# Routing stage of a two-block network on one core: choosing among 112 sums, dealing one-hot tiles singly, and moving three expert tiles and two weight loads

## The reference, cut to what matters

```python
def peer(h, wq, subkeys, u_tab, v_tab):          # 512 tokens, in blocks of 128
    q = (hb @ wq).reshape(128, 8, 2, 128)        # 8 heads, two halves
    s = einsum('thsd,snd->thsn', q, subkeys)     # 128 scores for each half
    s1, i1 = top_k(s[:, :, 0], 16)
    s2, i2 = top_k(s[:, :, 1], 16)
    cand = (s1[..., :, None] + s2[..., None, :]).reshape(..., 256)
    sc, ci = top_k(cand, 16)                     # 16 of 256 sums, for each head
    e1 = take_along_axis(i1, ci // 16); e2 = take_along_axis(i2, ci % 16)
    idx, gate = e1 * 128 + e2, softmax(sc)
    act = gelu(hb @ u_tab[idx].T) * gate
    return act @ v_tab[idx]
```

## Time and profile before

| | us |
|---|---|
| three runs | 4666.91, 4678.98, 4681.0 |
| median | 4678.98 |
| profiled execution: its own time | 4670.62 |
| its span | 4668.7 |
| first choice, VectorE, from 1096.1 | 39.8 |
| spreading, units 0 to 127 | 1137.9 to 1411.4: 273.5 |
| from there to the first `down` matmul | to 1445.9: 34.5 |

### The profile page before, as it was taken

The page is one execution under the profiler, slowest core; times in us unless marked ns, Lnnn a source line. Parts: engine busy times, 40 slices in busy tenths (PEclk is TensorE's granted clock), DMA queues, the critical chain, the costliest instruction groups (busy, mean ns, idle before and its releaser), DMA issues.

```text
span 4668.7 us, 51767 instructions
## 1 busy us (share of the span) xinstructions
PE 4338.2 (93%) x20942; PEld 3394.4 (73%) x20942; DVE 2612.5 (56%) x4338; ACT 1508.5 (32%) x2520; POOL 1928.1 (41%) x1031
## 2 busy tenths in 40 slices
PE   7878999998778999999999989988999989988999
PEld 3667755467666888888888877677888867756886
DVE  4675755458775888878645442653533450364334
ACT  3211311024773322222222232653222231353222
POOL 2244423134884555555555443104322236334443
PEclk9998999998889999999999999999999999999999
DMA  6200310332235454554554420001212212102321
GB/s 217 81 32 1 117 34 28 113 128 70 106 145 203 162 171 167 167 167 162 172 170 162 142 84 19 24 1 55 68 59 64 68 37 66 39 1 74 99 91 54
DMA packets 171050, 445.52 MB, mean 95 GB/s; under 512 B 12251, under 2 KB 79003, under 8 KB 167612
## 3 DMA queue, kind: packets, MB, share of 16 engines
q1 hardware_dynamic: 168060, 422.61, 27.1%
q0 software_dynamic: 2752, 19.60, 1.1%
HBM read 404.41 MB, written 37.75 MB: 95 GB/s over the span
## 4 chain that ended last, share of the span: by engine, by line
PE 71%; DVE 5%; ACT 4%; POOL 2%; issue 2%; DMA 0%; SPq 0%; POOLq 0%; ACTq 0%; DVEq 0%
PE psum L254 20%; PE psum L255 20%; PE psum L256 19%; PE psum L260 11%; PE psum L355 1%; POOL Pe L2579 1%; POOL Pd L2581 1%; DVE o L1591 1%; ACT o L1656 0%; ACT o L1659 0%; ACT stage L1665 0%; POOL pair L244 0%; DMA raw_ring<-peerv 0%; DVE oh L1560 0%; DVE ci L1542 0%
## 5 line engine op out<-in xcount | busy, mean ns | idle before, releaser
L244 POOL TENSOR_TENSOR pair<-raw_ring,pair 128x1024 fp32r<-128x1024 f32 x502 | 1304.5, 2607 | 1947.0 <-ACT pair L236 1894.4
L236 ACT CAST pair<-raw_ring 128x1024 fp32r<-128x1024 f32 x502 | 517.2, 1048 | 742.8 <-PE psum L256 687.6
L254 PE MATMUL psum<-pfh,pair 128*128 128x512 f32 x1152 | 459.8, 399 | 4.9 <-DVE pfl L1501 3.4
L255 PE MATMUL psum<-pfl,pair 128*128 128x512 f32 x1152 | 457.6, 397 | 0.0
L256 PE MATMUL psum<-pfh,pair 128*128 128x512 f32 x1152 | 452.6, 393 | 0.0
L1775 DVE SCALAR_TENSOR_TENSOR hlate<-psum,mods,hlate 128x512 f32<-128x512 f32 x512 | 367.1, 747 | 131.6 <-PE psum L256 129.7
L254 PE MATMUL psum<-Ah,pair 128*128 128x512 f32 x1024 | 402.3, 393 | 16.0 <-DVE Al L1769 16.0
L255 PE MATMUL psum<-Al,pair 128*128 128x512 f32 x1024 | 404.2, 395 | 0.0
L256 PE MATMUL psum<-Ah,pair 128*128 128x512 f32 x1024 | 398.0, 389 | 0.0
L254 PE MATMUL psum<-ffh,pair 128*128 128x512 f32 (+1 forms) x1056 | 377.6, 358 | 18.4 <-DVE ffl L1941 15.7
L255 PE MATMUL psum<-ffl,pair 128*128 128x512 f32 (+1 forms) x1056 | 377.0, 357 | 0.0
(11 more groups left out here) (616 smaller groups left out, 8848.6 us busy)
## 6 DMA issues: line engine op xcount, KB each, us to landing
raw_ring<-wmod SPq DMA_DIRECT2D x144, 512.0 KB, 5.4
raw_ring<-peeru SPq DMA_DIRECT2D x128, 512.0 KB, 3.5
raw_ring<-peerv SPq DMA_DIRECT2D x128, 512.0 KB, 3.8
gates<-stage SPq DMA_DIRECT2D x16, 2048.0 KB, 6.3
Gb<-gates SPq DMA_DIRECT2D x32, 1024.0 KB, 9.6
raw_ring<-win SPq DMA_DIRECT2D x48, 512.0 KB, 4.4
raw_ring<-wgate SPq DMA_DIRECT2D x44, 512.0 KB, 3.5
raw_ring<-wup SPq DMA_DIRECT2D x44, 512.0 KB, 3.5
```

The costliest lines, as they stand in the source:

```text
L236: ac.e.copy(self.pair(t)[0], k.R.of(t)).then_inc(*k.A.up("hi", t))
L244: po.e.tensor_tensor(lo, k.R.of(t), hi.bitcast(F), ALU.subtract).then_inc(*k.G.up("lo", t))
L254: e.matmul(out, w[0], x[0], start=first, stop=False, skip_group_check=True)
L255: e.matmul(out, w[0], x[1], start=False, stop=False, skip_group_check=True)
```

## The change

Four things change.

1. The choice looks at 112 sums of a head instead of 256: all 16 columns for the first four rows, and four columns for rows 4 to 15. They are made in sixteen smaller additions instead of eight. Since the place no longer is row times 16 plus column, nine small VectorE instructions work out row and column where four did; they are a piece of their own.
2. The owner of an `o1` tile is dealt for each token, not for each unit. `deal()` keeps a running load for each engine, adds to it the engine's other work of the unit, and gives each tile to the engine with the least.
3. Three U tiles (U8, U9, U10 behind units 2, 34 and 66) stay beside the spreading. U11 to U16 come after it.
4. SyncE loads V0 and V1 after the tenth store of gates, and V2 and V3 after the last store and ahead of loading the gates back.

```diff
-BESIDE = {2 + 16 * (n - FIRST): n for n in range(FIRST, EARLY)}
+BESIDE = {2: 8, 34: 9, 66: 10}
+CHOICE = 1.62
...
-            pe.wait_ge({"fused": G, "vector": V, "scalar": A}[own_o1(u)].at("o1", u, i2))
+            pe.wait_ge({"pool": G, "vector": V, "scalar": A}[OWN[4 * u + i2]].at("o1", u, i2))
...
-def own_o1(u):
-    if u >= 96:
-        return ("fused", "vector", "vector", "scalar", "fused", "vector", "vector")[u % 7]
-    i = u % 32 - u % 32 // 16
-    return "vector" if u % 16 == 15 else "scalar" if 13 * i % 30 < 13 else "fused"
+def deal():
+    cost, load, out = {"pool": 0.84, "scalar": 0.87, "vector": 0.29}, {"pool": 0.0, "scalar": 0.0, "vector": 0.0}, []
+    for u in range(128):
+        load["vector"] += CHOICE if u < 96 else 0.68
+        load["scalar"] += 0.58
+        if u in BESIDE:
+            load["scalar"] += 1.65
+            load["pool"] += 2.35
+        for i in range(4):
+            n = min(cost, key=lambda n: load[n] + cost[n])
+            load[n] += cost[n]
+            out.append(n)
+        if u == 95:
+            load = dict.fromkeys(load, 0.0)
+    return out
+OWN = deal()
...
-        for hd in range(8):
-            c = k.cand[:, 256 * hd:256 * hd + 256]
-            e.tensor_tensor(v3(c, 16), ... ALU.add)      # 16 x 16
-            if hd % 2:
-                yield
+        for lo, hi, w, at in ((0, 4, 16, 0), (4, 16, 4, 64)):
+            for hd in range(8):
+                o = c3[:, hd, at:at + w * (hi - lo)].rearrange("p (i j) -> p i j", j=w)
+                e.tensor_tensor(o, ... ALU.add)          # 4 x 16, then 12 x 4
+                if hd % 4 == 3:
+                    yield
...
-            if s == 0:
-                e.tensor_scalar(k.hiU, k.ci, 4, None, ALU.logical_shift_right)
-            else:
-                e.tensor_scalar(k.hiU, k.ci, 15, None, ALU.bitwise_and)
-            e.tensor_copy(k.hiF, k.hiU)
+        e.tensor_scalar(k.hiU, k.ci, 4, None, ALU.logical_shift_right)
+        e.tensor_copy(place, k.ci)
+        e.tensor_copy(row, k.hiU)
+        e.tensor_scalar(k.hiU, k.ci, 2, None, ALU.logical_shift_right)
+        e.tensor_copy(tmp, k.hiU)
+        e.scalar_tensor_tensor(out=row, in0=tmp, scalar=-12.0, in1=row, op0=ALU.add, op1=ALU.max)
+        e.tensor_scalar(tmp, row, 4.0, 48.0, ALU.mult, ALU.add)
+        e.scalar_tensor_tensor(out=tmp, in0=row, scalar=16.0, in1=tmp, op0=ALU.mult, op1=ALU.min)
+        e.tensor_tensor(place, place, tmp, ALU.subtract)
+        yield
...
-    for n in range(EARLY, AHEAD):                        # PE, ACT and POOL, behind the spreading
+    for n in range(FIRST + len(BESIDE), AHEAD):
...
         if ch == 0:
             R.load(sp, ("U", AHEAD - 1))
+        if ch == 9:
+            R.load(sp, ("V", 1))
+    R.load(sp, ("V", 3))
     sp.wait_ge(k.stl[0].at(8), k.stl[1].at(8))
```

More of the change, by code:

```diff
@@ L1517, in choose @@
         f4 = k.fidx[:, tt, :].rearrange("p (h s k) -> p h s k", h=8, s=2)
-        for hd in range(8):
-            c = k.cand[:, 256 * hd:256 * hd + 256]
-            e.tensor_tensor(v3(c, 16), bc(v4_[:, hd, 0, :], 2, [128, 16, 16]), bc(v4_[:, hd, 1, :], 1, [128, 16, 16]), ALU.add).then_inc(*V.up())
-            if hd % 2:
-                yield
-        groups = [tuple(x[:, w * hd:w * hd + w] for x, w in ((k.cand, 256), (k.best, 16), (k.ci, 16), (k.oh, 256))) for hd in range(8)]
+        c3 = v3(k.cand[:, 0:896], 112)
+        for lo, hi, w, at in ((0, 4, 16, 0), (4, 16, 4, 64)):
+            for hd in range(8):
+                o = c3[:, hd, at:at + w * (hi - lo)].rearrange("p (i j) -> p i j", j=w)
+                shape = [128, hi - lo, w]
+                e.tensor_tensor(o, bc(v4_[:, hd, 0, lo:hi], 2, shape), bc(v4_[:, hd, 1, 0:w], 1, shape), ALU.add).then_inc(*V.up())
+                if hd % 4 == 3:
+                    yield
+        groups = [tuple(x[:, w * hd:w * hd + w] for x, w in ((k.cand, 112), (k.best, 16), (k.ci, 16), (k.oh, 112))) for hd in range(8)]
         for half in (groups[0:4], groups[4:8]):
@@ L1547, in choose @@
         o4 = v4(k.oh, 16, 16)
-        for s in range(2):
-            if s == 0:
-                e.tensor_scalar(k.hiU, k.ci, 4, None, ALU.logical_shift_right).then_inc(*V.up())
-            else:
-                e.tensor_scalar(k.hiU, k.ci, 15, None, ALU.bitwise_and).then_inc(*V.up())
+        place, row, tmp = k.cand[:, 0:128], k.cand[:, 128:256], k.cand[:, 256:384]
+        e.tensor_scalar(k.hiU, k.ci, 4, None, ALU.logical_shift_right).then_inc(*V.up())
+        e.tensor_copy(place, k.ci).then_inc(*V.up())
+        dv.wait_ge(V.now())
+        e.tensor_copy(row, k.hiU).then_inc(*V.up())
+        dv.wait_ge(V.now())
+        e.tensor_scalar(k.hiU, k.ci, 2, None, ALU.logical_shift_right).then_inc(*V.up())
+        dv.wait_ge(V.now())
+        e.tensor_copy(tmp, k.hiU).then_inc(*V.up())
+        dv.wait_ge(V.now())
+        e.scalar_tensor_tensor(out=row, in0=tmp, scalar=-12.0, in1=row, op0=ALU.add, op1=ALU.max).then_inc(*V.up())
+        dv.wait_ge(V.now())
+        e.tensor_scalar(tmp, row, 4.0, 48.0, ALU.mult, ALU.add).then_inc(*V.up())
+        dv.wait_ge(V.now())
+        e.scalar_tensor_tensor(out=tmp, in0=row, scalar=16.0, in1=tmp, op0=ALU.mult, op1=ALU.min).then_inc(*V.up())
+        dv.wait_ge(V.now())
+        e.tensor_tensor(place, place, tmp, ALU.subtract).then_inc(*V.up())
+        yield
+        for s, which in ((0, row), (1, place)):
             dv.wait_ge(V.now())
-            e.tensor_copy(k.hiF, k.hiU).then_inc(*V.up())
-            dv.wait_ge(V.now())
-            e.tensor_tensor(o4, bc(v3(k.hiF, 16), 3, [128, 8, 16, 16]),
+            e.tensor_tensor(o4, bc(v3(which, 16), 3, [128, 8, 16, 16]),
                             k.row["i16"].unsqueeze(1).unsqueeze(1).to_broadcast([128, 8, 16, 16]), ALU.is_equal).then_inc(*V.up())
@@ L1591, in vector_route @@
         e.tensor_tensor(v3(k.o2[n], 128), *marks(k, u), ALU.is_equal).then_inc(*V.up("o2", u))
-        if own_o1(u) == "vector":
-            for i in range(4):
-                q = 4 * u + i
+        for i in range(4):
+            q = 4 * u + i
+            if OWN[q] == "vector":
                 e.tensor_scalar(k.o1[n][:, 128 * i:128 * i + 128], S["iota"], k.EG[0][:, q:q + 1], k.EG[2][:, q:q + 1], ALU.is_equal,
@@ L1652, in gates @@
         q = 4 * u
-        if own_o1(u) == "scalar":
+        mine = [i for i in range(4) if OWN[q + i] == "scalar"]
+        if mine:
             ac.wait_ge(V.at("EG", u // 32), P.at("sp", u - NO) if u >= NO else None)
-            for i in range(4):
+            for i in mine:
                 e.activation(o[i], k.sq["iota"], AF.Abs, scale=-1.0, bias=k.EG[0][:, q + i:q + i + 1]).then_inc(*A.up())
             ac.wait_ge(A.now())
-            for i in range(4):
+            for i in mine:
                 e.activation(o[i], o[i], AF.Relu, scale=k.EG[3][:, q + i:q + i + 1], bias=k.EG[2][:, q + i:q + i + 1]).then_inc(*A.up("o1", u, i))
@@ L1702, in pool_route @@
             W.lo(po, ("U", BESIDE[u]))
[L1703 to L1706, removed]
+        for i in range(4):
+            q = 4 * u + i
+            if OWN[q] == "pool":
+                po.wait_ge(V.at("EG", u // 32), P.at("sp", u - NO) if u >= NO else None)
                 e.tensor_scalar(k.o1[n][:, 128 * i:128 * i + 128], S["iota"], k.EG[0][:, q:q + 1], k.EG[2][:, q:q + 1], ALU.is_equal,
@@ L1827, in rounded @@
         e.copy(k.Ah[n % 4], k.pr[n % 3]).then_inc(*A.up("Ah", n))
-    for n in range(EARLY, AHEAD):
+    for n in range(FIRST + len(BESIDE), AHEAD):
         up(n)
```

## The result

The changed kernel takes 4624.65 us (median of four runs, 4621.01 to 4632.57), where the kernel before takes 4677.32 in the same runs: ratio 0.9882, 95% interval 0.9847 to 0.9917. I had said 4650 with a range of 4628 to 4668. The profiled execution took 4624.38 us, its span 4622.6, 46.1 less than before, twice the 21.8 that my terms add up to. (The medians differ by 52.7.)

What follows compares the result with a forecast made beforehand. TensorE was taken to bound the kernel (71% of the span), gains coming only where the chain leaves it. Terms -3.5 - 22 - 0.7 + 4.4 = -21.8 on 4670.6 gave 4648.8, stated as 4650, range 4628 to 4668.

Steps and rivals of the forecast that it cites:

- First choice, -3.5: First choice, ahead of the spreading: gate ready at 1132.3 instead of 1135.9, ScalarE's exponential ending last; -3.5 us, bounds -3 and -3.6.
- Blocks 0 to 2, -22: First three spreading blocks: 70.5 us each, -8 each and -6 for block 0; -22 us together, bounds -40 and -5.
- Only four units of buffers lie between engines: Blocks 0 to 2: reason for reckoning each block in three phases, 24.5, 24.0 and 17.5 us, sum 66.0.
- Taking away the second one: Blocks 0 to 2: removing a block's second U tile, in the slow phase, frees 0 to 2 us.
- Of which dealing gives little back: Blocks 0 to 2: first U tile costs 8.3 less 3.6 us, 4.7, and dealing recovers little of that.
- Block 3, -0.7: Last spreading block: VectorE drops to 59 tiles, GpSimd rises to 46, 38.9 us; -0.7 us, bounds -3 and +3.
- Handover, +4.4: Last spreading matmul (E) to first `down`: E+39.0 instead of E+34.5, six U tiles following; +4.4 us, bounds +2 and +9.
- Ports: Spreading: VectorE and GpSimd share ports; added cost to GpSimd at most some 4 us a block; wrong if its tile exceeds 1 us.
- Nothing left of it: Rival 1, blocks 0 to 2: queues stay out of step, blocks at 76, total 4670; chance 0.13.
- slower: Rival 2, blocks' first phase: VectorE's piece and other engines' tiles add, 24 us a block; 4685 at half; chance 0.06.
- half clock: Rival 4, blocks: TensorE's clock stays at 1.2 GHz, 3 us a block, 4659; chance 0.08.
- Even dealing works fully: Rival 3, spreading: `deal()` loads of 57.6 a block and 38.9 for the last hold, 4610; chance of below 4632: 0.13.

## Why the prediction was wrong, step by step

**First choice, -3.5: right**, -3.4, and for the reason given: the exponential behind the GELU of U7 ended last.

**Blocks 0 to 2, -22: this is the step that failed**, -46.9. I added up three phases, each at the pace of its slowest engine. In block 1 that gave 70.7 us, taken as 70.5, where 62.2 were measured; 7.1 of the difference lie in the third phase, 17.5 for 10.4. Three statements behind it went wrong.
- "Only four units of buffers lie between engines, so that a slow phase can't be averaged with a fast one." They can in part. GpSimd needs neither VectorE's `o2` nor its piece; in the slow phase it started 20 tiles where those 8 units hold 17. Three buffers instead of four cost 2.4 to 3.3 us a block, which shows that the lead counts.
- "Taking away the second one ... frees little (0 to 2)." Alone it freed 6.4 us in block 1, 6.1 of them in the third phase. With the tile there, GpSimd made a remainder in the slow phase (2.36 us) and stood still for TensorE as the third began (4.33). My check of the reckoning on the kernel before hid this: its third phase of 19.0 us looked like 11 units at 1.75 and was a stalled one.
- "Of which dealing gives little back." Undoing it costs 6.5 us a block on average, doing it alone gives 7.5. I had priced it at the 3.6 us of unit 34 and at nothing for the other turns. My block 1 went from 78.4 to 70.7 us by 3.4 for the shorter choice, 0.7 for the second U tile and these 3.6; alone the three measured 6.6, 6.6 and 7.5 a block.

What held: the middle phase (24.1 against 24.0), the first phase with its U tile (27.7 against 29.2), VectorE's shorter pieces, and GpSimd's load as the limit. For that limit I had taken 65 us a block as the far bound, though the text gave 63.5 for GpSimd's own work; it was 61.6. Three blocks at 65 are 38 us less than before, at 63.5 they are 43 less; measured were 46.9. So the bound -40 was too near.

**Block 3, -0.7: within its bounds**, +1.5. GpSimd is the bound there (40.90 of 41.70 busy), as the term had it, at 826 ns a tile. But 50 of its tiles start in this stretch, not 46: it had four of block 2 left when VectorE began block 3. A block bounded by VectorE's starts doesn't hold just its own tiles of GpSimd.

**Handover, +4.4: right in size** (+5.2; to `down` 39.8 us behind E where I had 39.0), with both gaps where they were put. The gap at U13 was 1.57 instead of 1. The `Gb` load was covered, by 10 us instead of 7: the gates came back 25.8 us behind E, not 28.

**Ports.** GpSimd's tile grew neither beyond 1 us nor at all in the changed kernel, 924 ns; so the shared ports of the Trainium skill's "SBUF — State Buffer", section "SBUF: two separate sides", show no added cost in the mean. Inside a block the cost is seen: in block 1 GpSimd's tiles take 0.81 us on average in the first phase, 1.19 beside VectorE's long passes and 0.80 in the third.

**Rivals.** "Nothing left of it", "slower" and "half clock" did not come; the granted clock rose in each of the blocks 0 to 2, from 0.75, 0.83 and 0.83 to 0.79, 0.89 and 0.87. "Even dealing works fully" (4610) was the nearest: the blocks came to 62 where `deal()` says 57.6. GpSimd's true cost of a tile, 0.92 with the long passes against the 0.84 that `deal()` uses, makes 5 us of difference for 66 tiles.

**What stays open.** How much of the 16 us a block belongs to which part has no single answer, since they overlap: alone 6.6, 7.5 and 6.6 us a block (choice, dealing, U tiles), undone 4.6, 6.5 and 5.8. What the early loads are worth with three U tiles behind the spreading was not isolated. Why the last store of gates landed later in some traces, and why block 2 varies by 2 us, was not tried.

## What to carry to other kernels

Before giving a phase its slowest engine's time, ask which other engines may run on in it: the sum over a block is bounded by the greatest total load of one engine, and that bound must be inside the range whenever an edit evens out the work. A part that only makes work fit together (dealing by tile instead of by unit) has no cost in any row; its price can be as much as the idle time of the bound engine, here 11.5 us a block, of which the dealing alone gave 7.5. And parts that remove the same idle time need not add: 56.6 us alone, 43.6 together in these traces.

## What the runs showed of the hardware

A copy of 128 columns on VectorE took ten times its usual time when GpSimd's subtraction of a weight tile (SBUF to SBUF) was running. VectorE, then GpSimd, in order of time in the first choice of the kernel after:

```profile
1108.16 0.23 DVE L1572 CAST cand<-hiU 128x128 f32<-128x128 uint32 x1
...
1108.68 2.32 DVE L1576 CAST cand<-hiU 128x128 f32<-128x128 uint32 x1
```

```profile
1108.45 2.46 POOL L244 TENSOR_TENSOR pair<-raw_ring,pair 128x1024 fp32r<-128x1024 f32 x1 [3.08 <-ACT pair L236]
```

The same copy two instructions earlier takes 0.23. The Trainium skill, "SBUF — State Buffer", section "SBUF: two separate sides", has the shared ports as an exclusive lock: whichever of the two engines starts first keeps them for its whole instruction. The trace agrees, since the copy ends 0.1 us behind the subtraction; that the copy ran in a mode that takes these ports is not shown. VectorE's one-hot tiles meet the same at units 2, 34 and 66, beside GpSimd's remainder: 2.38, 2.02 and 2.41 us for one tile, where the median is 0.34. An `o2`, which reads one of its inputs from PSUM, was not held up: in the kernel before one began at 1222.68, inside a remainder (1222.03 to 1224.39), and took 0.67 as always. I had priced the nine small instructions at 0.26 each; one of them in such a place costs as much as all the others. It was hidden here by the wait for the exponential.
